# Wider value projections, latent projections nearer to their norms, and a rotation of both token blocks at once, in a two-block transformer kernel

## The reference, cut to what matters

```python
h = rms_norm(x, attn_norm)                       # first block
sb_q, sb_k, sb_v, cq, ckv, k_pe = split(h @ w_in)      # 512, 512, 512, 384, 256, 32 columns
sb = stick_breaking_attention(sb_q, sb_k, sb_v)        # 8 heads of 64
q  = rms_norm(cq, cq_norm) @ w_uq                      # 8 heads of 96
k_nope, v = split(rms_norm(ckv, ckv_norm) @ w_ukv)
q, k = rope(rms_norm(q, q_norm)), rope(rms_norm(concat(k_nope, k_pe), k_norm))   # last 32 of 96
mla = chunk_causal_softmax_attention(q, k, v)
...
q_l, k_l, v_l, f_l = split(h_l @ w_in)           # second block, layer 0: 768, 768, 768, 256 columns
q_c, k_c, v_c, f_c = split(h_c @ w_in)           # the same weights on 256 context tokens
o = diff_attend(rope(q_l), concat(k_c, rope(k_l)), concat(v_c, v_l), lam)
...
a, g = split(h @ pw1_w + pw1_b)                  # second block, layer 1: 1024 and 1024 columns
u = depthwise_conv(a * sigmoid(g), dw_w)         # 31 taps
```

## Time and profile before

| | |
|---|---|
| median of 3 runs | 1994.74 us (1993.57 to 1997.96) |
| the profiled execution | 1994.48 us, its span 1992.7 us |
| busy in the span | PE 1820.2, DVE 940.0, ACT 873.8, POOL 856.7 us |
| mean granted clock of TensorE | 0.965 of full |

### The profile page before, as it was taken

One profiled execution on the slowest core, in us unless ns is written; L12 is line 12 of the kernel. 1 busy time (PEld: TensorE's weight loads), 2 busy tenths in 40 slices (PEclk: granted clock), 3 DMA queues, 4 the chain that ended last, 5 costly groups with the idle time before them and its releaser, 6 DMA issues.

```text
span 1992.7 us, 37237 instructions
## 1 busy us (share of the span) xinstructions
PE 1820.2 (91%) x13992; PEld 1664.1 (84%) x13992; DVE 940.0 (47%) x1569; ACT 873.8 (44%) x1315; POOL 856.7 (43%) x432
## 2 busy tenths in 40 slices
PE   6998899999999988999999978996799978879997
PEld 5886798999999877788888877964699978569997
DVE  2564239650000477566666634245444456634444
ACT  4354254555555455454554542133244444324443
POOL 3400369897888899000000044200355546015552
PEclk8999899999999999999999988988899989989999
DMA  5363454554555578655555541100355533035553
GB/s 201 96 241 125 142 171 159 177 168 158 179 182 185 197 262 261 203 191 194 194 191 195 194 156 64 64 11 9 117 181 180 187 130 127 22 106 182 181 186 106
DMA packets 85340, 312.67 MB, mean 157 GB/s; under 512 B 9601, under 2 KB 9601, under 8 KB 84865
## 3 DMA queue, kind: packets, MB, share of 16 engines
q1 hardware_dynamic: 84960, 309.41, 46.8%
q0 software_dynamic: 288, 1.97, 0.3%
HBM read 310.29 MB, written 1.05 MB: 156 GB/s over the span
## 4 chain that ended last, share of the span: by engine, by line
PE 82%; POOL 7%; DVE 5%; issue 3%; ACT 2%; DMA 1%; DVEq 0%; SPq 0%; POOLq 0%; ACTq 0%
PE psr L670 42%; PE acc L917 18%; PE acc L670 6%; PE psr L659 5%; POOL sq L2008 4%; POOL wl L484 3%; PE psr L897 2%; PE acc L730 1%; PE psr L646 1%; PE psr L1062 1%; DVE rinv L1528 1%; ACT wh L475 1%; DVE sq L1547 1%; PE psr L985 1%; PE psr L766 1%
## 5 line engine op out<-in xcount | busy, mean ns | idle before, releaser
L484 POOL TENSOR_TENSOR wl<-ring,wh 128x1024 fp32r<-128x1024 f32 x286 | 710.9, 2489 | 617.8 <-ACT wh L475 617.4
L475 ACT ACTIVATE wh<-ring 128x1024 fp32r<-128x1024 f32 x458 | 482.4, 1055 | 558.9 <-PE psr L670 497.4
L670 PE MATMUL psr<-hh,wh 128*128 128x256 f32 x2200 | 554.3, 288 | 63.6 <-DVE hl L1561 60.8
L670 PE MATMUL psr<-hl,wh 128*128 128x256 f32 x2200 | 550.8, 287 | 0.0
L670 PEld LDWEIGHTS psr<-hh,wh 128*128 128x128 f32 x2200 | 431.7, 196 | 69.0 <-issue 65.1
L670 PEld LDWEIGHTS psr<-hl,wh 128*128 128x128 f32 x2200 | 431.8, 196 | 0.5 <-issue 0.2
L670 PE MATMUL psr<-hh,wl 128*128 128x256 f32 x2200 | 311.9, 285 | 9.7 <-POOL wl L484 9.7
L484 DVE TENSOR_TENSOR wl<-ring,wh 128x1024 fp32r<-128x1024 f32 x172 | 213.1, 1239 | 176.7 <-ACT wh L475 176.7
L670 PEld LDWEIGHTS psr<-hh,wl 128*128 128x128 f32 x2200 | 286.0, 193 | 11.9 <-POOL wl L484 11.9
L2013 POOL DMA_DIRECT2D arena<-in_consts x1 | 0.8, 757 | 360.0 <-DVE x L1810 360.0
L917 PE MATMUL acc<-wh,hh 128*128 128x512 f32 x512 | 137.2, 390 | 1.5 <-ACT wh L475 1.5
(11 more groups left out here) (269 smaller groups left out, 2407.0 us busy)
## 6 DMA issues: line engine op xcount, KB each, us to landing
ring<-in_peer_u SPq DMA_DIRECT2D x128, 512.0 KB, 3.2
ring<-in_peer_v SPq DMA_DIRECT2D x128, 512.0 KB, 3.2
ring<-in_ada_w SPq DMA_DIRECT2D x96, 512.0 KB, 4.4
ring<-in_ffn_a SPq DMA_DIRECT2D x44, 512.0 KB, 3.9
ring<-in_ffn_b SPq DMA_DIRECT2D x44, 512.0 KB, 3.3
ring<-in_ffn_d SPq DMA_DIRECT2D x44, 512.0 KB, 3.3
ring<-in_pw SPq DMA_DIRECT2D x24, 512.0 KB, 3.3
ring<-in_w_in SPq DMA_DIRECT2D x18, 512.0 KB, 3.7
```

Source lines behind the costliest of these rows:

```text
L475: nc.scalar.activation(wh[:, q % 2, :], ring[:, s, :], ACT.Copy).then_inc(high_ready, 1)
L484: eng.tensor_tensor(wl[:, q % 2, :], ring[:, n % NS, :], wh[:, q % 2, :], ALU.subtract)\
L670: return mm(out, w, a, start=start, stop=stop, skip_group_check=True)
```

## The change

1. `split_tokens` takes several tiles whose 1024 columns are ordered by rows of the weight matrix: two chunks of 128 input features by 512 columns (`in` 4 and 5 as four tiles, `ev` 2 to 5), or four chunks by 256 columns (`ev` 0 and 1). Each matmul moves 512 (or 256) columns. The host orders the weights so (`_by_rows`).
2. Second block: columns 512 to 767 go through two `psr` banks, columns 0 to 511 through the four `acc` banks; ACT copies the latter after the last tile, and TensorE waits for these copies (`values_in`) before the first output product.
3. First block: `uq` comes right after norm 2, `in` 1 after it, then `ukv`, `in` 2, `in` 3 and the values. The roots move in ACT's queue: the first before the drain of `in` 1, the second before the drain of `in` 3. TensorE no longer waits for the drain of `in` 5 before the attention, but at its first output product.
4. DVE rotates both token blocks in one set of six operations of 256 elements.
5. `conv_order` keeps `pw1` three chunks ahead of `rep` in place of two: `pw1` 0 to 5, `rep` 3, `pw1` 6, `rep` 4, `pw1` 7, `conv` 3, `rep` 5, `conv` 4, ...
6. SP's release of a slot that held one of these tiles is unchanged (they are split tiles); two branches that were never reached are removed.

```diff
-    order = [("pw1", c) for c in range(PE_CONV[0] + 2)]
+    order = [("pw1", c) for c in range(PE_CONV[0] + 3)]
     for c in PE_CONV[:-1]:
-        order += [("rep", c)] + ([("pw1", c + 2)] if c + 2 < KC else [])
+        order += [("rep", c)] + ([("pw1", c + 3)] if c + 3 < KC else [])
...
-    g = [("lam",), ("norm", 0), ("in", 6), ("in", 7), ("in", 8), ("norm", 1), ("in", 0), ("norm", 2), ("in", 1)]
-    g += uq + [("in", 2)] + ukv + [("in", 3), ("in", 4), ("in", 5)]
+    g = [("lam",), ("norm", 0), ("in", 6), ("in", 7), ("in", 8), ("norm", 1), ("in", 0), ("norm", 2)]
+    g += uq + [("in", 1)] + ukv + [("in", 2), ("in", 3), ("in", 4), ("in", 5)]
...
+            def split_tokens(tiles, width, blocks):
+                at_k, starts = 0, range(0)
+                for n in tiles:
+                    per = SLOT // width
...
+                    split_product(n, [(out, slice(j * width, (j + 1) * width),
+                                       *(x_[:, tb * P:(tb + 1) * P] for x_ in parts(at_k + j)))
+                                      for out, _, parts, tb in blocks for j in range(per)],
+                                  starts if n == tiles[0] else (), weights_move=True)
+                    at_k += per
...
-            for c in (3, 4, 5):
-                project_in(c)
+            project_in(2)
+            project_in(3)
+            banks = [bank(("in", 4 + tb)) for tb in range(TB)]
+            split_tokens([TILE_NO["in", 8 + m] for m in range(4)], 512,
+                         [(banks[tb][:, :], tb, h_parts, tb) for tb in range(TB)])
             drained(pe, ("in", 3))
-            drained(pe, ("in", 5))
...
-            for c in range(3):
-                split_tokens("ev", c, [(("v2", c), h_parts), (("vc", c), hc_parts)])
+            split_tokens([TILE_NO["ev", m] for m in range(2)], 256,
+                         [(ps[:, tb * T:(tb + 1) * T], what, parts, tb) for what, parts, ps in banks for tb in range(TB)])
+            split_tokens([TILE_NO["ev", 2 + m] for m in range(4)], 512,
+                         [(acc[2 * s + tb][:, :], (s, tb), parts, tb) for s, parts in enumerate((hc_parts, h_parts))
+                          for tb in range(TB)])
...
+                if c in (1, 3):
+                    head_roots(c // 2)
                 ps = full(act, ("in", c))
...
+            used(act, TILE_NO["ev", 5])
+            for s in range(4):
+                A(vall[:, s, 0:512], acc[s][:, :], ACT.Copy).then_inc(values_in, 1)
...
-                for tb in range(TB):
-                    x1, x2 = src[:, tb, :, NOPE:NOPE + 16], src[:, tb, :, NOPE + 16:QKD]
+                x1, x2 = src[:, :, :, NOPE:NOPE + 16], src[:, :, :, NOPE + 16:QKD]
```

More of the change, by code:

```diff
@@ L222 @@
 LAST_TILE |= {(k, c): TILE_NO[k, 2 * c + 1] for k, n in (("in", 9), ("pq", 8), ("pw1", 8)) for c in range(n)}
[L223 to L224 removed]
+LAST_TILE |= {(g, c): TILE_NO[k, 2 * c + 1] for g, k in (("k", "ek"), ("kc", "ek"), ("q", "eq")) for c in range(3)}
+LAST_TILE["in", 4] = TILE_NO["in", 11]
+LAST_TILE |= {(g, "B"): TILE_NO["ev", 1] for g in ("v2", "vc")}
 LAST_TILE["f", 0] = TILE_NO["ef", 1]
@@ L442, in build @@
         rotated = sem("rotated")
+        values_in = sem("values_in")
         neg_max2 = sem("neg_max2")
@@ L699, in split_features @@
                 return banks[0][0]
[L701 to L709, removed]
+            def split_tokens(tiles, width, blocks):
+                at_k, starts = 0, range(0)
+                for n in tiles:
+                    per = SLOT // width
+                    if n == tiles[0]:
+                        first = {}
+                        for q, (out, bank_no, parts, tb) in enumerate(blocks):
+                            first.setdefault(bank_no, q * per)
+                        starts = first.values()
+                    split_product(n, [(out, slice(j * width, (j + 1) * width),
[3 more added lines that the diff above has]
+                    at_k += per
             def h_parts(k):
@@ L838, in _ @@
                     pe.wait_ge(sb_probs, three + 1)
+                    if three == 0:
+                        drained(pe, ("in", 4))
+                        drained(pe, ("in", 5))
                     outputs(acc[1], lambda tb: sbv[:, tb, 64 * three:64 * three + 64], two["pa"][:, three % 2, :], three)\
@@ L976, in _ @@
                 split_features("ek", c, [(("k", c), h_parts), (("kc", c), hc_parts)])
-            for c in range(3):
-                split_tokens("ev", c, [(("v2", c), h_parts), (("vc", c), hc_parts)])
+            banks = [(what, parts, bank((what, "B"))) for what, parts in (("v2", h_parts), ("vc", hc_parts))]
+            split_tokens([TILE_NO["ev", m] for m in range(2)], 256,
[3 more added lines that the diff above has]
+                          for tb in range(TB)])
             pe.wait_ge(rotated, 2)
@@ L997, in _ @@
                     drained(pe, ("aT", 2 * i + 1))
+                    if i == 0:
+                        pe.wait_ge(values_in, 4)
                     for s in range(4):
@@ L1403, in _ @@
                 drains(A(kall[:, 2 * c:2 * c + 2, 0:T], ps[:, :].rearrange("p (h t) -> p h t", h=2), ACT.Copy), ("kc", c))
-            for c in range(3):
-                highs_after(("ev", 2 * c), ("ev", 2 * c + 1))
-                ps = full(act, ("v2", c))
-                drains(A(vall[:, 2:4, c * T:(c + 1) * T], ps[:, :].rearrange("p (b n) -> p b n", b=2), ACT.Copy), ("v2", c))
-                ps = full(act, ("vc", c))
-                drains(A(vall[:, 0:2, c * T:(c + 1) * T], ps[:, :].rearrange("p (b n) -> p b n", b=2), ACT.Copy), ("vc", c))
+            highs_after(("ev", 0), ("ev", 1))
+            for what, s in (("v2", 2), ("vc", 0)):
+                ps = full(act, (what, "B"))
+                drains(A(vall[:, s:s + 2, 512:768], ps[:, :].rearrange("p (b n) -> p b n", b=2), ACT.Copy), (what, "B"))
+            highs_after(("ev", 2), ("ev", 3))
+            used(act, TILE_NO["ev", 5])
+            for s in range(4):
+                A(vall[:, s, 0:512], acc[s][:, :], ACT.Copy).then_inc(values_in, 1)
             for i in range(2 * H2 + 3):
```

51 lines of the change are left out of this document (21 added, 30 removed).

## The result

The changed kernel takes **1961.32 us** (median of 4 runs, 1959.13 to 1962.01) where the kernel before took 1995.68 beside it (1993.57 to 1997.96): ratio **0.9824**, 95% interval 0.981 to 0.9838. That is 34.4 us; 41.2 were forecast, and 1961.3 lies outside the range, which ended at 1958.5. The profiled execution took 1960.77 us, its span is 1958.9.

A forecast was written before the change was run, and what follows sets the result against it. It took TensorE's own stream to bound the kernel (82% of the chain). First block -9.0, second -30.4, convolution -1.8 sum to -41.2 against the profiled 1994.48: 1953.3 us, range 1948.5 to 1958.5.

The forecast's parts named there:

- The paces: Value stages, both blocks: a matmul takes 0.227 us for 512 columns, 0.120 for 256, 0.112 for 128, at clock 1.00.
- the columns rule: Value stages: matmuls paced by columns alone, so at most 1 us gained; 1994 us, chance 0.01.
- The second block: Second block's values: -31.1 us by pace, +0.75 for ACT's further copies; sum -30.4, bounds -31.5 and -29.
- The +0.5 for ACT's two drains: First block, after the last value matmul: both value banks drained there delay ACT's copy; +0.5 us.
- The rotation: First block: rotating both token blocks at once saves DVE some 1 us, hidden behind ACT's copy; 0.
- Which waits would go in the convolution: Convolution: DVE gains its waits for sigmoids 5 and 7, 4.8 us, loses 3.0 to POOL's splits; net -1.8.
- the rival in which the wide matmuls themselves pull it down: Value stages: wide matmuls pull TensorE's clock to 0.50; slower, 2004 us for 20 us at that clock; chance 0.01.
- the lock term: First block's values: one DVE scaling ahead of a POOL split stops TensorE, +0.8 us; two would cost 2.2.
- The wait before `uq`: First block's order: `uq` waits for DVE's last `apply` of the norm, which `in` 1 had covered; +0.35 us.
- The modulation tiles behind them arrive one per split, before the attention asks: nothing: First block's values to attention: transfers of the modulation tiles cause no wait; 0 us.
- -10.6 in the pace: First block's values: 48 matmuls at 0.227 us, 10.9 us, for 192 at 0.112, 21.5 us; -10.6 us.
- POOL and DVE shut each other out: First block: three splits held back, keys ready only at 105 or later, 3 us lost; 1956.3 us, chance 0.15.

The follow-up runs named there:

- e8: Changed kernel with the second block's values as in the kernel before (six products of 128 columns, their banks and drains); 1988.88 us, ratio 0.9968.
- e16: Changed kernel with DVE rotating each token block of the first block by itself again; 1961.34 us, ratio 0.982.
- e2: Changed kernel with the convolution's old order, `pw1` two chunks ahead; 1956.24 us, ratio 0.9827.
- e0: Changed kernel run again without any edit; 1955.73 us, ratio 0.9835.
- e15: Changed kernel without DVE's two scalings of k in the first block, so the attention uses unscaled k; 1958.04 us, ratio 0.982.
- e4: Changed kernel with the second rotation's root asked of ACT ahead of the two splits that stood before it; 1955.07 us, ratio 0.9804.
- e1: Changed kernel with the whole first block undone (old values, order and rotation); 1962.53 us, ratio 0.985.
- e9: Changed kernel with only the first block's values back to 128-column products; new order and rotation stay; 1963.38 us, ratio 0.9831.
- e14: Changed kernel plus 16 unread filling products at the first attention's start and 40 ahead of its output projection; 1954.86 us, ratio 0.98.
- e17: Changed kernel plus only 40 unread filling products ahead of the first attention's output projection; 1958.05 us, ratio 0.9798.
- e6: Changed kernel with both the edit of e4 and the edit of e5; 1960.18 us, ratio 0.9847.
- e13: Changed kernel plus 16 unread filling products in TensorE's pause at the first attention's start; 1955.24 us, ratio 0.9806.
- e7: Changed kernel with each modulation pair of the first block's attention one round later; 1958.92 us, ratio 0.9818.
- e11: Changed kernel run again without any edit; 1958.01 us, ratio 0.9811.
- e5: Changed kernel with ACT copying the first modulation pair's rows ahead of its table load and first-round exponentials; 1958.46 us, ratio 0.9815.

## Why the prediction was wrong

**Right, by its own steps.** The paces: 0.227 us for 512 columns, 0.120 for 256, at clock 1.00, in both blocks; the columns rule, by which nothing would be gained, is refuted once more by 33.45 us for 64.40. The second block: 31.0 in the stage, the first exponential 3.4 us after the last value matmul (1286.98 against 1283.56; forecast 3.4), 30.9 in the whole by e8. The +0.5 for ACT's two drains: last value matmul to the second pair 4.36 us for 3.87. The rotation: 0 (e16). Which waits would go in the convolution: both went, and the mean is set by DVE's last tap. Its size: 1.6 us by two pairs of profiles for 1.8, while the medians of e2 and e0 show 0.5 and cannot tell the two apart. With the clock at 1.00 in both value stages, the rival in which the wide matmuls themselves pull it down did not come.

**Wrong in size.** "One scaling ... ahead of a split uses up the 0.9 to spare and stops TensorE for about 0.8, two for 2.2 ... I take one: +0.8" is the lock term. e15 measures it at 1.8, and the values take 12.85 to 12.87 us in every profile that has their new shape, DVE's scalings and the second root at its place: not one scaling but two scalings and a rotation step fall beside the last splits. The forecast weighed this case (two cost 2.2) and chose the other. The Trainium skill, "SBUF — State Buffer", section "Who interferes with whom", has the rule by which the engine that starts first holds the shared ports to its end. The trace agrees (a scaling 3.75 us for 1.76), and e4 shows the part that a sum of durations does not: in a chain of dependent steps each one can lose a start, 2.2 us at a time. The wait before `uq` was 0.5 on average for 0.35.

**The step that failed.** "The modulation tiles behind them arrive one per split, before the attention asks: nothing", and with it the silent assumption that the attention behind costs what it cost before, plus the 0.5 for ACT's drains. In the first profile the attention took 71.3 us for 65.0. A transfer stands on the chain for 6.52 us, TensorE waits 1.4 us in all for tiles, and it works 10.2 us at 0.50, which can cost 5.1. With the clock at 1.00 the attention takes 65.3 to 66.5 us, 0.8 more than before on average: 0.5 the drains, the rest waits for the ring. When the clock falls to 0.50 in its first rounds it takes 68.0 to 71.9, on average 4.4 more than without. That happened in 8 of 17 profiles with the new values, in 2 of the 7 with the first block as changed, and in none of 3 with the old values (before, e1, e9). Three are too few to show that the change brings the falls: with even odds each, none in three is one case in eight. That a fall follows stands of TensorE is shown by e14 and e17 ahead of the output projection, and e4 and e6 have one right behind their stand of 3.1 us before `uq`. Which stand does it in the attention stays open: the waits for the ring precede the fall in the first profile and e13, but none precedes it in e0, e4, e7, e15 and e16, and e1, e2, e8 and e11 have such waits and no fall; the pause for ACT's copy, or the wait in its place, precedes it in six profiles and is there without such a fall in eight.

**The account.** First block: -10.6 in the pace became 8.7 in the stage (10.5 without the lock, by e15's 11.07), less 0.5 before `uq`, less 0.9 in the attention at full clock and, averaged over the seven profiles with the changed first block, 1.1 by the clock: about -6.2, and e1 and e9 have 6.8 and 5.4. Second block -30.2, convolution -1.6. Together -38.0, and the four comparisons average 36.9. So the forecast of 41.2 was 3 too high by its terms: 1.0 the lock, 1.5 the attention (0.4 waits for tiles, 1.1 clock), the rest in small pieces. In the first profile, 7.4 us short of the forecast by its span, the attention alone has 5.8 of it and the lock 1.0.

The rest of the first result is chance. The same program run again had medians of 1955.7, 1958.0 and 1954.2 us, beside 1992.4, 1995.8 and 1993.0 for the kernel before: all three lie inside the stated range, which had "some 2 us of run-to-run spread", and the first result does not. That does not make the terms right: each gain is still under the forecast. The rival "POOL and DVE shut each other out" (1956.3) was nearest in kind, but what it asks for did not come: the keys were ready at 103.8, not at 105 or later, and no wait for a split reached 1 us.

## What to carry to other kernels

A stage that gets shorter keeps its neighbours' work: list what runs beside it (splits, scalings, transfers for the next stage) and divide by the new length, not the old. Moving a stage's work off a collision can move it into a longer one (e4), and a pause filled at one place may only return at the next (e5); look for what ends the round before reordering. When one profile shows a stretch at half clock or a late transfer, profile the same program again before explaining it: here the same stage of the same program took 65.6 to 71.3 us.

## What the runs showed of the hardware that had not been expected

Small shifts decide how many steps of a DVE chain meet a split of POOL: three steps took 3.41 us when one of them met a split and 5.56 when two did, and POOL's splits had started 0.3 us earlier against the chain (0.06 us behind its first step in e4, 0.34 in the first profile). So in a tuned schedule an edit can win or lose 2 us by a shift upstream that it was not made for.

The granted clock takes a sizeable part of this kernel: the records at 0.50 sum to 131 to 155 us per execution. TensorE is busy in 74 to 95 us of that, so 37 to 48 us is an estimate of what they cost at most. The same 128 products take 27.89 us at full clock and 29.3 to 30.9 where the clock falls at their start.
